# A streamed encoder trunk: the low parts of all weight units on VectorE, none on GpSimd

## The reference

```python
mem_n = rmsnorm(mem, mem_norm)
for i in range(4):
    kind, j = i % 3, i // 3
    h = rmsnorm(x, norm_mix[i])
    proj = h @ w_in[kind][j]
    mix_in, xq = proj[..., :-1024], proj[..., -1024:]
    # 0: mamba2_mixer (conv, chunked scan), 1: differential_attention, 2: spatial gating
    mix_out = mixer[kind](mix_in, ...)
    cross = memory_cross_attention(xq, mem_n, w_mem_kv[i], xq_norm[i], xk_norm[i])
    x = x + jnp.concatenate([mix_out, cross], axis=-1) @ w_out[kind][j]
    h = rmsnorm(x, norm_ffn[i])
    x = x + jnp.square(jax.nn.relu(h @ w_ff1[i])) @ w_ff2[i]      # 1024 -> 4096 -> 1024
```

## Time and profile before

| | |
|---|---|
| median of 3 runs | 2078.13 us (2077.42 to 2080.14) |
| the profiled execution | 2077.48 us, its span in the trace 2075.7 us |
| TensorE, matmuls | 1879.0 us busy, 91% of the span |
| VectorE | 1059.1 us, 51% |
| ScalarE | 979.3 us, 47% |
| GpSimd | 718.6 us, 35% |
| granted TensorE clock, mean | 0.961 of full speed |
| loaded | 302.91 MB, 146 GB/s over the span |

### The profile page before, as it was taken

How to read it: one execution, slowest core, us unless ns; L and a number is a source line. 1 busy time by engine, 2 the same in 40 slices (tenths; PEclk the granted TensorE clock), 3 DMA queues, 4 the chain that set the end, 5 groups by cost and what they waited for, 6 DMA issues and landing times. The chain is left out here.

```text
span 2075.7 us, 29795 instructions
## 1 busy us (share of the span) xinstructions
PE 1879.0 (91%) x10596; PEld 1632.8 (79%) x10596; DVE 1059.1 (51%) x1677; ACT 979.3 (47%) x1512; POOL 718.6 (35%) x289
## 2 busy tenths in 40 slices
PE   4899788999999996899997999999899888888998
PEld 3799667789987775789986877998789766678886
DVE  4546756355437674454346434544544756534432
ACT  4555544444545553355444444544454554344443
POOL 2243211334444320334443323444343321232443
PEclk9899999999999998999999999999999999998999
DMA  4454321545564441445563534555355322153553
GB/s 170 142 181 152 114 81 41 178 152 189 182 200 155 143 143 40 144 150 185 192 202 135 171 122 150 178 188 191 125 187 177 111 93 82 71 172 117 178 182 122
DMA packets 83751, 305.69 MB, mean 147 GB/s; under 512 B 9264, under 2 KB 9520, under 8 KB 83632
## 3 DMA queue, kind: packets, MB, share of 16 engines
q1 hardware_dynamic: 83344, 302.95, 42.9%
q10 hardware_dynamic: 288, 1.05, 0.1%
HBM read 302.91 MB, written 1.05 MB: 146 GB/s over the span
## 5 line engine op out<-in xcount | busy, mean ns | idle before, releaser
L609 POOL TENSOR_TENSOR w_lo_t<-raw,w_hi_t 128x1024 fp32r<-128x1024 f32 x285 | 718.4, 2521 | 1340.0 <-ACT w_hi_t L879 1339.5
L879 ACT ACTIVATE w_hi_t<-raw 128x1024 fp32r<-128x1024 f32 x570 | 597.0, 1058 | 762.8 <-PE ps L659 418.0
L1080 DVE TENSOR_TENSOR w_lo_t<-raw,w_hi_t 128x1024 fp32r<-128x1024 f32 x285 | 425.2, 1502 | 572.1 <-ACT w_hi_t L879 572.1
L672 PE MATMUL ps<-hT_hi,w_hi_t 128*128 128x256 f32 x1536 | 441.7, 288 | 19.0 <-DVE w_lo_t L1080 10.8
L673 PE MATMUL ps<-hT_lo,w_hi_t 128*128 128x256 f32 x1536 | 439.6, 286 | 0.0
L674 PE MATMUL ps<-hT_hi,w_lo_t 128*128 128x256 f32 x1536 | 439.4, 286 | 0.0
L657 PE MATMUL ps<-w_hi_t,act_hi 128*128 128x512 f32 x832 | 328.3, 395 | 19.4 <-DVE w_lo_t L1080 17.5
L658 PE MATMUL ps<-w_lo_t,act_hi 128*128 128x512 f32 x832 | 325.7, 392 | 0.0
L659 PE MATMUL ps<-w_hi_t,act_lo 128*128 128x512 f32 x832 | 325.6, 391 | 0.0
L672 PEld LDWEIGHTS ps<-hT_hi,w_hi_t 128*128 128x128 f32 x1536 | 300.1, 195 | 22.7 <-issue 19.7
L673 PEld LDWEIGHTS ps<-hT_lo,w_hi_t 128*128 128x128 f32 x1536 | 300.3, 196 | 0.9
(11 more groups left out here) (185 smaller groups left out, 1961.3 us busy)
## 6 DMA issues: line engine op xcount, KB each, us to landing
raw<-in_wstream SPq DMA_DIRECT2D x570, 512.0 KB, 3.8
mix<-in_mem SPq DMA_DIRECT2D x1, 1024.0 KB, 5.0
x<-in_x SPq DMA_DIRECT2D x1, 1024.0 KB, 11.9
out<-x SPq DMA_DIRECT2D x2, 512.0 KB, 3.1
wsT<-in_sgu_wT ACTq DMA_DIRECT2D x1, 512.0 KB, 5.2
sgain<-in_sgu_gain ACTq DMA_DIRECT2D x1, 512.0 KB, 5.8
consts_sb<-in_consts SPq DMA_DIRECT2D x1, 448.0 KB, 5.7
percol_sb<-in_percol SPq DMA_DIRECT2D x1, 225.5 KB, 5.7
```

Source lines behind the costliest of these rows:

```text
L609: return pool.tensor_tensor(w_lo_t[:, slot, :], raw[:, slot, :], w_hi_t[:, slot, :].bitcast(F32), ALU.subtract)
L672: pe.matmul(o, wh[:, k, c], act[0][:, kt, :], start=kt == 0 and f % 2 == 0, stop=False, skip_group_check=True)
L879: act.activation(w_hi_t[:, u % RING, :], raw[:, u % RING, :], ACT.Copy).then_inc(w_hi, 1)
L1080: dve.tensor_tensor(w_lo_t[:, u % RING, :], raw[:, u % RING, :], w_hi_t[:, u % RING, :].bitcast(F32), ALU.subtract)\
```

## The change

GpSimd's block is taken out; its program does nothing any more after the start. `lo_to` on VectorE now goes through all units, even and odd, in their order, at the same places as before. The two semaphores for even and odd low parts stay, and with them every wait of the other engines. The lines behind the block move up by 14: L1080 is now L1066, L1132 is L1118, L1096 is L1082.

```diff
-        @block.gpsimd
-        def _(pool):
-            def lo(slot):
-                return pool.tensor_tensor(w_lo_t[:, slot, :], raw[:, slot, :], w_hi_t[:, slot, :].bitcast(F32), ALU.subtract)
-            with pool.Fori(0, NU // RING) as it:
-                for s in range(0, RING, 2):
-
-                    pool.wait_ge(w_hi, it * RING + (s + 1))
-                    lo(s).then_inc(w_lo[0], 1)
-            for u in range(NU // RING * RING, NU, 2):
-                pool.wait_ge(w_hi, u + 1)
-                lo(u % RING).then_inc(w_lo[0], 1)
...
-            odd = [1]
+            low = [0]
 
             def lo_to(n):
 
-                while odd[0] < min(n, NU):
-                    u = odd[0]
+                while low[0] < min(n, NU):
+                    u = low[0]
                     dve.wait_ge(w_hi, u + 1)
                     dve.tensor_tensor(w_lo_t[:, u % RING, :], raw[:, u % RING, :], w_hi_t[:, u % RING, :].bitcast(F32), ALU.subtract)\
-                        .then_inc(w_lo[1], 1)
-                    odd[0] += 2
+                        .then_inc(w_lo[u % 2], 1)
+                    low[0] += 1
```

## The result

The changed kernel takes 2097.84 us (median of 4 runs, 2097.18 to 2099.51), the kernel before 2078.14 in the same comparison. The ratio is 1.0094 with a 95% interval of 1.0077 to 1.0112: slower by about 0.9%. The forecast was 2095.5, in a range of 2079 to 2112.

The account below looks back on a forecast made before the run. The prediction took TensorE's work (1879.0 us, 91% of the span) and its idle moments as the bound. Terms summing to +17.6 us gave 2095.7 for the median, stated as 2095.5 us, range 2079 to 2112.

Parts of the forecast that it names:

- start, to unit 9: At the kernel's start, VectorE's small operations return to short times and TensorE's wait of 7.09 us shrinks: −5.9 us.
- layer 0, SSM and out projection: In layer 0's mixer, last low parts come late as in layer 3 before: +9.9 and +0.6, together +10.5 us.
- six norms: At the ends of mixer and feed-forward in layers 0 to 2, the last low part comes late: 6 × 2.2 = +13.2 us.
- layer 1, DIFF, with its group norm and out projection: In layer 1, last low parts stand behind head norms or scores on VectorE, with some low-clock cost: +18.3 us.
- layer 2, SGU: In layer 2, the wait of 9.3 us before unit 309 becomes 7.9 before unit 308: −1.3 us.
- layer 3, SSM and out projection: In layer 3's mixer, the wait of 5.72 us falls to 1.5 and a small dt wait goes: −7.8 us.
- layer 3, feed-forward: In layer 3's feed-forward, eight waits on low parts of 3.4 us go, as these then take 1.22: −9.4 us.
- Contention ends: At the start and in layer 3, GpSimd no longer holds VectorE's operations up: −5.9, −7.8 and −9.4 us.
- The last unit is late in layers 0 to 2: A product's last low part, now VectorE's, stands behind its work on the product before: +10.5, +13.2, +18.3, −1.3 us.
- clock rival: Every new wait of 2 us or more brings a low-clock unit, at norms (+14) and DIFF (+6): about 2115 us, chance 0.10.
- faster rival: VectorE, rid of contention, catches up everywhere in layers 0 to 2, leaving only reliefs of −26: about 2052 us, chance 0.08.
- Feed-forward, 0: In the feed-forward of layers 0 to 2, low parts still come in time, with thin cover: no change, 0 us.

Follow-up runs that it names:

- e1_spare: Changed kernel, with GpSimd subtracting a 128x1024 tile into one nobody reads, once per even unit from 176 to 416: 2125.63 us, 1.0215 times the kernel before.
- e5_layer3: Change made in layer 3 alone: GpSimd keeps the even units below 418, VectorE makes all from 418 on: 2062.35 us, 0.9917 times the kernel before.
- e3_norms: Changed kernel, with GpSimd making six low parts, the last units of the products at the norms: 2079.11 us, 0.9989 times the kernel before.
- e7_diff: Changed kernel, with GpSimd making six low parts in layer 1's DIFF, the last of their products: 2077.41 us, 0.9987 times the kernel before.
- e9_ssm0: Changed kernel, with GpSimd making nine low parts in layer 0, last units of SSM and out projection: 2080.14 us, 0.9996 times the kernel before.
- e4_margin: Changed kernel, with each low part placed one unit earlier in VectorE's queue and none on GpSimd: 2038.11 us, 0.9788 times the kernel before.
- e8_few: Changed kernel, with GpSimd making 39 low parts: 34 last units TensorE waited for and five others: 1999.83 us, 0.9609 times the kernel before.
- e6_swap: Kernel before with the halves exchanged: GpSimd makes all odd units, VectorE the even ones: 2193.66 us, 1.0544 times the kernel before.
- e2_last_unit: Changed kernel, with GpSimd making 143 low parts, every product's last unit and unit 417: 2015.76 us, 0.9684 times the kernel before.

## Why the prediction was right, step by step

The terms of the sum against the difference of the traces. Each is the change of a stretch's length, from the start of a unit on TensorE to that of another, so that idle time and clock are in it:

| term | forecast | measured |
|---|---|---|
| start, to unit 9 | −5.9 | −7.0 |
| layer 0, SSM and out projection | +10.5 | +9.2 |
| six norms | +13.2 | +16.4 |
| layer 1, DIFF, with its group norm and out projection | +18.3 | +16.2 |
| layer 2, SGU | −1.3 | −0.6 |
| layer 3, SSM and out projection | −7.8 | −6.4 |
| layer 3, feed-forward | −9.4 | −8.0 |
| sum | +17.6 | +19.8 |

The misses of the single terms come to 11 us without their signs and to 2.2 with them. Each term has the right sign and about the right size, but that the total came so near is in part luck.

- **Contention ends:** right, shown by e1_spare and e5_layer3. Its size over the whole kernel I had too small: VectorE is busy 1234.0 us where I said near 1290. Most of it lay where nobody waited.
- **The last unit is late in layers 0 to 2:** right, shown by e3_norms, e7_diff and e9_ssm0. The waits came within 0.3 us of the sums made from the rows of before. Some of these sums were about 0.1 too high: the rows give 1.92 at the norm, where I wrote 2.0, and 3.96 and 2.88 in DIFF, where I wrote 4.1 and 3.0; measured are 1.82, 3.93 and 2.91.
- **Start:** the part that I didn't have is unit 0, which begins 0.9 earlier and runs at full speed now (2.84 us instead of 4.0). The wait at unit 7 is 3.13 (forecast "some 3").
- **Norms:** the wait is 1.82 each, 10.9 in all, as worked out. What was mis-sized is what follows it: I gave 0.2 for each, and it is 0.9 on average. In two of the six (units 296 and 348) the late unit ran at a lower clock, 4.41 us instead of 2.72; after the filler unit 169 took 3.68 instead of 2.84.
- **DIFF:** six waits of 15.2 us in all (forecast 15.6), low-clock units in three of them.
- **Layer 3:** the small gains are as forecast, −1.8, −6.4 and −9.3. Against them stand 1.6 in the SSM and 1.3 in the feed-forward, which the sum didn't have: units at a lower clock, now that the waits have another pattern. They are why both of layer 3's terms are too good.
- **The clock rival** was partly true: low-clock units cost some 4 us at the norms and 3 in layer 3 that I hadn't granted, where the rival wanted 20. After the same wait of 1.82 us, four of six units ran at full speed and two didn't. Which ones can't be told from the length of the wait. My argument against this rival, full speed after a wait of 2.94 us, held for one place only: in the changed kernel units 48 and 457 waited 3.0 and 3.1 us and took 4.6 us each, where 457 took 3.1 before. Nor does a first matmul tell the clock of its unit: 7, 204, 296 and 348 began with 0.47 or 0.49 and ran slow.
- **The faster rival** failed at the place named for it: VectorE does not catch up before the last units. The rule of the Trainium skill's GPSIMD Engine Reference (Engine selection) is right on the price of one operation, 1.22 us against 2.34, and says nothing on whether that price is paid on the path. With e4_margin or e8_few, VectorE does make nearly all of them, and the time falls as the rule would have it.
- **Feed-forward, 0:** right, and e6_swap shows that it was so because the contention went with the same edit.

Two forecasts behind the prediction missed widely: e6_swap, since I priced collisions by their number in the kernel before, and e2_last_unit, since the layer that I took as undisturbed wasn't. e3_norms and e4_margin each gained more than forecast.

## What to carry to other kernels

When work is moved from a slow idle engine to a fast busy one, ask of each piece what stands ahead of it in the new queue and when its consumer wants it; 21 of 570 equal pieces here held more than the whole effect. A half-and-half split by index lets an accident of parity decide: give the helper the pieces that would be late and nothing more, since everything else that it does can lengthen the main engine's operations. Where one layer of a kernel already has the order that a change gives to the others, its trace is the best template, once it is asked what the other layers lose today.

## What the runs showed of the hardware

One subtraction of 128x1024 on GpSimd can hold up a VectorE operation of any size: 128x2 operations go from 0.16 to 1.80 and 2.34 us. In the kernel before it did so to all but one of the operations that started while GpSimd's ran and took two tensors, or a tensor_scalar's one, from SBUF. The five reductions that started so kept their times. Who starts first decides (VectorE, then GpSimd):

```profile
459.14 2.56 DVE L1143 TENSOR_TENSOR rf<-rf 128x1024 f32<-128x1024 f32 x1 [2.62 <-ACT rf L958]
475.49 1.22 DVE L1080 TENSOR_TENSOR w_lo_t<-raw,w_hi_t 128x1024 fp32r<-128x1024 f32 x1
...
458.22 2.40 POOL L609 TENSOR_TENSOR w_lo_t<-raw,w_hi_t 128x1024 fp32r<-128x1024 f32 x1 [3.36 <-ACT w_hi_t L879]
476.29 2.69 POOL L609 TENSOR_TENSOR w_lo_t<-raw,w_hi_t 128x1024 fp32r<-128x1024 f32 x1 [4.15 <-ACT w_hi_t L879]
```

The square (L1143) starts 0.92 us into GpSimd's operation and takes 2.56 instead of 1.22. It ends 1.08 after GpSimd's. This happened to 24 of its 32, so 32 of the 81 us on VectorE's other work are the feed-forward's squares. The low part at 475.49 was under way when GpSimd's began: it keeps its 1.22, and GpSimd's takes 2.69. Of the low parts, all 61 that started during an operation of GpSimd's were held up. Operations that read a tensor from PSUM (ps) were not, though 24 of the 64 hT_lo and 8 of the 32 sums onto x started so (ns, min/median/max):

```profile
L1110 DVE SCALAR_TENSOR_TENSOR hT_lo<-ps,percol_sb,hT_hi x64: 472/476/486, 62.3 to 1877.9; 128x256 fp32r<-128x256 f32 x64
L1319 DVE TENSOR_TENSOR x<-ps,x x32: 678/681/692, 425.7 to 2070.6; 128x512 f32<-128x512 f32 x32
```

Held up are also tensor_scalar operations, which have a single tensor as input: L1046, 2.03 at 128x2 and 2.35 at 128x16, and the pair L1099, from 1.42 to 3.47. The Trainium skill (SBUF — State Buffer, Who interferes with whom) exempts operations with at most one input in SBUF outside of the two-port modes, and names tensor_scalar as one that can enter such a mode; the trace agrees for the operations on PSUM and shows the hold-up for tensor_scalar even at two elements per partition. I hadn't expected that over the kernel these meetings make 166 us of 1059.

TensorE's clock answered equal waits of 1.82 us unequally: the late unit took 2.83 to 2.85 us four times and 4.41 twice, counted to where the next unit would begin. The windows from first to last matmul of units 168 and 296 in the changed kernel show it. Their values stand as in the earlier trace rows, and the granted clock behind the five engines is 1.00 of full speed in the one and 0.63 in the other:

```profile
639.74:642.75 3.01, 3.01 (x14) 2.44 (x15) 3.01 (x3) 0.00 (x0) 0.00 (x0) 1.00 0.63 192
1116.62:1121.19 4.57, 4.57 (x14) 3.58 (x15) 3.26 (x3) 0.00 (x0) 0.00 (x0) 0.63 0.77 226
```
